# One 512-column pass for two halves: high weights meet the high and the low part of the activations together

## The reference

```python
def half_ffn(x, shift, scale, gate, g, w_gate, w_up, w_down):
    h = rmsnorm(x, g) * (1 + scale) + shift
    return x + 0.5 * gate * swiglu(h, w_gate, w_up, w_down)   # 1024 -> 2816 -> 1024
# layer 0: half_ffn, then Fourier and neighbourhood attention with w_out, then half_ffn
# layer 1: half_ffn, then latent (MLA) attention with w_o, then half_ffn; rmsnorm at the end
x_l = x_l + mod_l[:, 5] * y_l          # y_l = concatenated heads @ w_out, or @ w_o
```

## Time and profile before

| | us |
|---|---|
| median of 3 runs | 3292.5 (3287.77 to 3293.3) |
| the profiled execution, its own time | 3279.74 |
| its span, first to last instruction | 3277.6 |
| PE busy in the span | 2987.5 |
| DVE busy | 2356.1 |
| ACT busy | 1022.8 |

### The profile page before, as it was taken

One profiled execution on the slowest core, in us unless ns is written; L12 is line 12 of the kernel. 1 busy time (PEld: TensorE's weight loads), 2 busy tenths in 40 slices (PEclk: granted clock), 3 DMA queues, 4 the chain that ended last, 5 costly groups with the idle time before them and its releaser, 6 DMA issues. The chain is left out here.

```text
span 3277.6 us, 43558 instructions
## 1 busy us (share of the span) xinstructions
PE 2987.5 (91%) x15744; PEld 2395.9 (73%) x15744; DVE 2356.1 (72%) x4780; ACT 1022.8 (31%) x2039; POOL 1290.9 (39%) x1213
## 2 busy tenths in 40 slices
PE   8999899886877999989987999859999999999999
PEld 5877566564644587757665776639997999996898
DVE  5776777777877776787777877777754887846574
ACT  2423211111231242231111111135455544444443
POOL 1105777776767211577666666660000010000000
PEclk9999999998888999989998999969999999999999
DMA  9659999999999867999999999987661787742352
GB/s 352 226 200 370 377 409 409 409 409 385 395 352 389 333 231 269 368 381 409 409 406 408 395 409 409 404 321 239 225 226 42 256 278 242 254 156 90 123 182 102
DMA packets 276501, 1003.55 MB, mean 306 GB/s; under 512 B 31952, under 2 KB 32752, under 8 KB 276032
## 3 DMA queue, kind: packets, MB, share of 16 engines
q0 software_dynamic: 173696, 635.85, 50.5%
q1 hardware_dynamic: 100944, 361.15, 30.9%
q10 hardware_dynamic: 1648, 3.78, 0.3%
HBM read 999.57 MB, written 1.05 MB: 305 GB/s over the span
## 5 line engine op out<-in xcount | busy, mean ns | idle before, releaser
L288 PE MATMUL bank<-hT,ring 128*128 128x256 f32 x3744 | 838.5, 382 | 10.0 <-ACT hT L928 7.2
L288 PEld LDWEIGHTS bank<-hT,ring 128*128 128x128 f32 x3744 | 716.0, 192 | 139.3 <-issue 33.0
L414 POOL DMA_INDIRECT gring<-in_expert_u,idx x512 | 592.6, 1157 | 307.3 <-issue 146.5
L414 POOL DMA_INDIRECT gring<-in_expert_v,idx x512 | 599.9, 1172 | 277.1 <-issue 146.1
L584 PE MATMUL bank<-gring,dg 128*128 128x512 f32 x1012 | 526.0, 666 | 140.3 <-DMA gring<-in_expert_v,idx 121.2
L1387 DVE CUSTOM_DVE_ANT_0 gring<-gring,t_tok 128x1024 f32<-128x1024 f32 x512 | 601.2, 1222 | 20.2 <-DMA gring<-in_expert_u,idx 10.6
L1362 DVE SCALAR_TENSOR_TENSOR x<-gring,wts,x 128x1024 f32<-128x1024 f32 x259 | 333.0, 1286 | 279.0 <-DMA gring<-in_expert_v,idx 169.9
L1696 DVE TENSOR_TENSOR wl<-ring,wr 128x1024 fp32r<-128x1024 f32 x309 | 377.5, 1223 | 211.2 <-ACT wr L1691 210.7
L584 PEld LDWEIGHTS bank<-gring,dg 128*128 128x128 f32 x1012 | 209.7, 214 | 393.9 <-issue 359.4
L1700 PE MATMUL bank<-hr,wr 128*128 128x258 f32 (+1 forms) x1512 | 430.0, 284 | 1.5 <-DVE hl L2165 0.7
L1702 PE MATMUL bank<-hr,wl 128*128 128x258 f32 (+1 forms) x1512 | 426.6, 282 | 0.0
(11 more groups left out here) (327 smaller groups left out, 3697.7 us busy)
## 6 DMA issues: line engine op xcount, KB each, us to landing
ring<-in_stream SPq DMA_DIRECT2D x679, 512.0 KB
lat_ada<-in_ada POOLq DMA_DIRECT2D x66, 512.0 KB, 5.3
t_tok<-in_ada POOLq DMA_DIRECT2D x56, 512.0 KB, 5.2
gring<-in_ada POOLq DMA_DIRECT2D x56, 512.0 KB, 5.8
gring<-in_expert_u,idx POOLq DMA_INDIRECT x512
gring<-in_expert_v,idx POOLq DMA_INDIRECT x512
na_bias_sb<-in_na_bias POOLq DMA_DIRECT2D x1, 4096.0 KB, 15.2
x<-in_x SPq DMA_DIRECT2D x2, 512.0 KB, 4.3
```

What stands on the lines that cost most here:

```text
L288: last = pe.matmul(out, w[:, k * P:(k + 1) * P], act_T[:, k, :], start=(k == 0), stop=(k == KD - 1))
L414: pool.indirect_dma_start(out=gring[:, N % GR, :], out_offset=None, in_=table, in_offset=bass.IndirectOffsetOnAxis(ap=idx[:, b, 4 * (Q % 3 ...
```

## The change

The two matmuls that use `wr` are made one. High and low parts of an activation become halves of one tile (`hh0`, `hh1`, `ff`), and `pe_pair` sends both, 512 columns, through one matmul into a whole bank: high in columns 0 to 255, low in 256 to 511. The third matmul (`wl` x high) adds into columns 0 to 255. The residual then adds both halves: first gate x columns 256 to 511, then, after a wait on the semaphore `l_part`, gate x columns 0 to 255. Only the down and output projections use `pe_pair`; the projections behind a norm, and the ones in MLA's query, keep `pe_three`.

```diff
         def dve_residual(dve, R, m):
...
-            dve.scalar_tensor_tensor(out=hT[:, m, :], in0=bank[4 + m % 2][:, 0:S],
-                                     scalar=mods[:, L, (3 * j + 2) * KD + m, LAT:LAT + 1], in1=hT[:, m, :], op0=ALU.mult,
-                                     op1=ALU.add).then_inc(l_res, 1)
+            gate = mods[:, L, (3 * j + 2) * KD + m, LAT:LAT + 1]
+            dve.scalar_tensor_tensor(out=hT[:, m, :], in0=bank[4 + m % 2][:, S:2 * S], scalar=gate, in1=hT[:, m, :],
+                                     op0=ALU.mult, op1=ALU.add).then_inc(l_part, 1)
+            dve.wait_ge(l_part, 8 * R + m + 1)
+            dve.scalar_tensor_tensor(out=hT[:, m, :], in0=bank[4 + m % 2][:, 0:S], scalar=gate, in1=hT[:, m, :],
+                                     op0=ALU.mult, op1=ALU.add).then_inc(l_res, 1)
...
+        def pe_pair(pe, bk, s, i, both, start, stop):
+            cols = slice(i * P, (i + 1) * P)
+            pe.matmul(bk[:, :].rearrange("p (two t) -> p two t", two=2), wr[:, s % SPLIT, cols], both[:, :, 0:S], start=start,
+                      stop=False)
+            return pe.matmul(bk[:, 0:S], wl[:, s % SPLIT, cols], both[:, 0, 0:S], start=False, stop=stop)
...
-                    last = pe_three(pe, bank[4 + m % 2][:, 0:S], s0 + 44 + d, i, fr[:, k, :], fl[:, k, :], k == 0, k == KF - 1)
+                    last = pe_pair(pe, bank[4 + m % 2], s0 + 44 + d, i, ff[:, k], k == 0, k == KF - 1)
...
-                    hi, lo = (yr[:, k, 0:S], yl[:, k, 0:S]) if k < 4 else (hr1[:, k - 4, 0:S], hl1[:, k - 4, 0:S])
-                    last = pe_three(pe, bank[4 + st % 2][:, 0:S], LAB_O + st, k, hi, lo, i == 0, i == KD - 1)
+                    last = pe_pair(pe, bank[4 + st % 2], LAB_O + st, k, hh1[:, (k + 4) % KD], i == 0, i == KD - 1)
...
-                pe_unit_three(pe, M_O + st, bank[4 + st % 2][:, 0:S], [hr1[:, k, 0:S] for k in range(KD)],
-                              [hl1[:, k, 0:S] for k in range(KD)])
+                pe.wait_ge(w_low, M_O + st + 1)
+                for k in range(KD):
+                    last = pe_pair(pe, bank[4 + st % 2], M_O + st, k, hh1[:, k], k == 0, k == KD - 1)
+                last.then_inc(sp_used, 1)
...
-        hr0 = sb(ctx, "hr0", [P, KD, SX], F32R)
-        hl0 = sb(ctx, "hl0", [P, KD, SX], F32R)
+        hh0 = sb(ctx, "hh0", [P, KD, 2, SX], F32R)
...
-            fr = sb(for_ffn, "fr", [P, KF, S], F32R)
-            fl = sb(for_ffn, "fl", [P, KF, S], F32R)
+            ff = sb(for_ffn, "ff", [P, KF, 2, S], F32R)
```

More of the change, by code:

```diff
@@ L1727, in pe_normed_unit @@
         def pe_normed_unit(pe, n, u, out):
-            pe_unit_three(pe, u, out, [high[n][:, k, :] for k in range(KD)], [low[n][:, k, :] for k in range(KD)])
-        def pe_unit_three(pe, u, out, a_high, a_low):
             pe.wait_ge(w_low, u + 1)
             for k in range(KD):
-                last = pe_three(pe, out, u, k, a_high[k], a_low[k], k == 0, k == KD - 1)
+                last = pe_three(pe, out, u, k, high[n][:, k, :], low[n][:, k, :], k == 0, k == KD - 1)
             last.then_inc(sp_used, 1)
@@ L2232, in program @@
             "mla_roped", "mla_kv_mm", "mla_kv"))
-        stored, l_fin = sem("stored"), sem("lat_weighted")
+        stored, l_fin, l_part = sem("stored"), sem("lat_weighted"), sem("lat_residual_low")
         a_or, ab_yl, m_cr, m_cl = (sem(n) for n in ("att_out_high", "fft_low", "mla_cq_high", "mla_cq_low"))
@@ L2246, in program @@
             lat_ada = sb(for_condition, "lat_ada", [P, 4, UW])
-        hr1 = sb(ctx, "hr1", [P, KD, SX], F32R)
-        hl1 = sb(ctx, "hl1", [P, KD, SX], F32R)
+        hh1 = sb(ctx, "hh1", [P, KD, 2, SX], F32R)
+        hr0, hl0, hr1, hl1 = hh0[:, :, 0, :], hh0[:, :, 1, :], hh1[:, :, 0, :], hh1[:, :, 1, :]
         late = {n: sb(ctx, n + "_sb", list(io[n].shape)) for n in ("mla_gq", "rope", "rotm", "final_g")}
@@ L2267, in program @@
             turned = sb(for_mla, "turned", [P, 2, S])
+        fr, fl = ff[:, :, 0, :], ff[:, :, 1, :]
         lab_u, lab_q, lab_k = lab[:, 0:4, :], lab[:, 4:12, :], lab[:, 12:16, :]
```

## The result

The changed kernel takes 3299.5 us (median of 20 runs, 3288.6 to 3306.8), the kernel before 3291.4 (20 runs, 3282.7 to 3299.1). The ratio is 1.0024 with a 95% interval of 1.0015 to 1.0034. In microseconds that is +8.2 where +5.5 was forecast: slower, by a little more than the 6.6 us set as the mark for "no measurable change", and the interval lies on both sides of that mark. It is also just above the +3 to +8 us that the forecast gave itself, and inside its whole range (3286 to 3309).

The account below looks back on a forecast made before the run. PE was taken to bound down projections F = 0, 2 and 3, DVE F = 1, a DVE-ACT residual chain the output projections. 13.0 us for 25 residuals minus 7.5 (616 x) gave +5.5, 3298 us; range 3286 to 3309.

Parts of the forecast that it names:

- The residual's chains: Output projections: a chain round DVE and ACT, once a tile, goes from 3.85 to 4.37 us with the second residual instruction.
- the steep price: Rival: the 512-column matmul leaves one column a cycle, 60 ns lost on each product, about +50 us; chance 0.03.
- x: What one product saves on PE in down and output projections: 12.1 ns, from 356.3 to 344.2 ns.
- The residual, 25 times 0.52 us: Down and output projections: 25 residuals on the path, each 0.52 us longer as two dependent instructions, 13.0 us.
- I take 12.1 ns as paid once by each matmul: Products in down and output projections: fixed 12.1 ns a matmul beyond its columns, so a 512-column pass takes 225.4 ns.
- The two columns more of the earlier trace: 258-column matmuls start 119.6 ns apart, against 118.75 at 256: 0.85 ns for two columns, read as a cycle each.
- rival of a cost by columns: Rival: the pass costs by its columns, 235 ns, x = 2.6, +11.4 us; chance 0.25 together with nothing saved.
- The buffers are the same bytes in another order ... cost nothing: Moved tiles: no DMA, wait or copy added on ACT, SP or POOL, weights still early; cost nothing.
- the hidden load: Rival: weight load was the limit and is now hidden, pass 216 ns, x = 21.5, -0.2 us; chance 0.18.
- a change that does nothing (x = 0): Rival: three passes' worth of time in two instructions, +13.0 us, 3305.5; within the 0.25 for columns or nothing saved.
- a residual pair that overlaps: Rival: residual pair costs 0.40 us, with x = 21.5 gives -3.2 us; chance 0.06 for faster by 3 or more.

Follow-up runs that it names:

- the reordered kernels: ACT's weight copy moved earlier: output projections only, kernel before 0.9978, changed 0.9977; down projections and last tiles too, three matmuls 0.9959, change in most tiles 0.9932.
- tiles alone: Kernel before with only the change's tiles (high and low part as halves of one tile), three matmuls and one residual instruction kept; ratio 0.9990.
- changed, one residual instruction: Changed kernel without the residual instruction that adds columns 256 to 511; ratio 0.9982, latent stream 14.8 us under the changed kernel.
- halves apart: Changed kernel with the down projections' activations in rows of 258 columns, 256 used, so halves aren't side by side; latent stream 1079.4 us, not timed as ratio.
- changed kernel reordered: Changed kernel with ACT's weight copy ahead of the high part and square in both output projections; ratio 0.9977.
- fewer columns: Changed kernel, down projections' pass at 512, 512, 384, 320 columns in F = 0 to 3; pass means 230.5, 173.1, 145.1 ns at 512, 384, 320; no ratio.
- F = 1 and the last tiles freed too: Copy moved ahead in down and output projections, last tile's residual earlier, change's tiles; against kernel before 0.9959 with three matmuls, 0.9932 with the change except each stage's last tile.

## Why the prediction was right or wrong

The forecast was +5.5 us with a range that holds the result. The residual's chains, the main cost, were right; PE's gain was mis-sized, and the moved tiles were put at nothing. The range is as wide as all the rivals but the steep price, so that it held says little. By stage, each from the end of one stage's last residual to that of the next (starts read from both traces); the forecast from the prediction's own terms with x = 12.1 ns:

| | forecast | measured |
|---|---|---|
| up and down projection F = 0 | -1.6 | -1.9 |
| layer 0's mixer and output projection | +4.1 | +4.0 |
| F = 1 | +2.2 | +1.9 |
| F = 2 | -1.6 | -1.2 |
| MLA and its output projection | +4.1 | +5.6 |
| F = 3 and the end | -1.6 | -1.2 |
| sum | +5.5 | +7.2 |

*The residual, 25 times 0.52 us.* Right in its size (3089.03 to 3089.54, then 3090.06) and its places: 4.37 us a tile as predicted, the stretch of F = 1 at 38.10 with 38.1 predicted, PE's idle time behind a down projection up by 0.54. Shown from both sides, by adding an instruction to the kernel before (+11.8 for a cheaper one) and taking it from the changed one (-14.8, of which 1.5 is the clock). That the cause is the chain and not DVE's load is shown by the reordered kernels, for the output projections and for F = 1.

*"I take 12.1 ns as paid once by each matmul".* This step failed. The pass takes 230.6 ns and not 225.4, the matmul behind it 120.3 and not 118.75, and x is 4.8 (0.42 us in 88 products of F = 0) to 5.1. The two columns more of the earlier trace rows were too short a lever: over the whole stream 258 columns take 120.1 ns on the mean and in the new tiles 119.2, so place alone moves that distance by as much as the two columns were to show. A fixed price came out near the means at 320 and 384 columns, but not at 512, and at 384 it is 8 ns in one pattern and 21 in the other. With x = 4.8 the prediction's sum gives 13.0 - 3.0 = +10.0 us, near the rival of a cost by columns (+11.4 at 2.6 ns), which had 235 ns for the pass. The measured 230.6 lies halfway between the two.

*"The buffers are the same bytes in another order ... cost nothing".* This failed too, in the other direction. The new tiles alone make the stream 2.3 us shorter, 0.87 in each up projection, none of which has an edited instruction. In the changed kernel, whose down projections no longer have the matmuls that the new place slows, the placement is worth 4 x 0.87 = 3.5 us, and the sum is 10.0 - 3.5 = 6.5. The two errors, 4.5 us too much gain on PE and 3.5 us of placement not seen, have opposite signs. That the total came within 2 us of the measured one is in good part luck.

*The granted clock, 0.7 us.* Between 6.5 and the measured 7.2 lies the granted clock, which is not the same in the two executions. The MLA stage took 1.5 us more than forecast. None of its own instructions differ but the output projection's. Its stretches at a clock of 0.50 (1.2 GHz; columns as in the earlier trace rows) are one in the kernel before and two in the changed one. The one before, and the second of the changed one, come at the end of an idle time of PE of 4.26 us or just behind it; the first of the changed one is behind F = 2.

```profile
2973.20:2976.60 3.40, 3.27 (x4) 1.51 (x5) 1.12 (x4) 0.60 (x1) 0.00 (x0) 0.50 0.00 0
```

```profile
2951.20:2954.60 3.40, 3.40 (x18) 3.40 (x18) 0.06 (x1) 0.00 (x0) 0.00 (x0) 0.50 0.39 146
2992.10:2995.50 3.40, 3.40 (x6) 1.69 (x5) 0.62 (x3) 1.19 (x2) 0.00 (x0) 0.50 0.00 0
```

The stage's length goes with them in the other kernels too, when 8 x 0.52 = 4.2 us is taken off where the residual has two instructions:

| | stage, us | less residual | at 0.50, us |
|---|---|---|---|
| before | 142.9 | 142.9 | 3.4 |
| changed, one residual instruction | 142.9 | 142.9 | 3.4 |
| tiles alone | 144.2 | 144.2 | 6.8 |
| changed | 148.6 | 144.4 | 6.8 |
| halves apart | 149.4 | 145.2 | 10.2 |

In the four kernels with another order it is 138.1 us with 3.4 at 0.50, 139.9 and 140.0 with 6.8, and 140.5 with 10.2.

So the 1.5 us are the clock's. In the other direction, the stream's first 10 us had a mean granted clock of 0.74 before and 0.82 in the changed kernel, an estimated 0.8 us less (10 x 0.08). 6.5 + 1.5 - 0.8 = 7.2.

*What stays open.* In the changed kernel PE is idle 1.82 us behind F = 2, busy again from 2950.79, and its clock falls at 2951.20. It falls in that place in the other kernels with this idle time or more too (halves apart and the changed kernel reordered, 1.83 and 1.82 us; fewer columns, 2.74). Before, PE is idle 1.28 us there, and with the added residual instruction alone 1.74, and in neither does the clock fall there. It doesn't either behind F = 0 in the changed kernel, after the same 1.82. So the MLA stage's 1.5 us may belong to the change, by way of the longer idle time; no run tests it. Nor is the cause of the beat known, or why the new tiles speed up the products of 258 columns.

The rivals: the hidden load (216 ns) and the steep price fall by the 230.6 ns; a change that does nothing (x = 0) falls by the 0.42 us that the pass saves in F = 0's stretch; a residual pair that overlaps falls because its second half starts after the end of the first (3089.54, and 3089.03 + 0.48). The cost by columns has the wrong price for the pass, and its total of +11.4 would have been nearer to the +10.0 that the residuals and the true x give than the forecast was.

The Trainium skill's rule for the isolated distance ("TensorE: Matmul & The Clock Gate", "Back-to-back issue gap") would have 216 ns at 512 columns; the fp32r pass measured here, 224 to 235 ns and 230.6 on the mean, does not follow it.

## What to carry to other kernels

Before merging matmuls, count what the merge adds on the engine that reads the result, and walk the chain there: an instruction of half a microsecond costs its full time wherever tiles hand over one by one, and nothing beside a bound engine. Here 832 saved matmuls, worth 5 ns each, were paid with 25 such instructions. If the chain is the bound, first take out of it what needn't be there (the weight copy in front of `wl`); the merge pays only after that. Here it took all three places: with the output projections alone in the new order the change still gave nothing in the timed ratios, and with F = 1 and the last tiles freed too it gave some 3.4 to 4.6 us.

## What the runs showed of the hardware

- An fp32r matmul with its own weight load costs more than its columns at 2.4 GHz, and not by a fixed amount: 256 columns 118.7 ns on the mean, 320 from 140 to 153, 384 either 168 or 181, 512 224 to 235. Which of the values holds can change where an fp32 matmul has come between, with the same tiles and lengths. Plain fp32 records of 256 columns (L288) had 215 or 216 ns nearly throughout, where the granted clock was 1.00.
- Two tiles woven into one, with the same instructions, changed the 258-column products by 0.75% (115.27 to 114.40 us for 320 of them), the same 0.87 us in each of the four up projections and in all eight kernels here that have these tiles. The 256-column products got slower in the same tiles (33.03 to 33.10 us for the stretch of F = 0 with 88 products).
- `scalar_tensor_tensor` on 128x256 from PSUM took 0.42 us with a constant scalar and 0.48 with one read from a tile.
- Short stretches at a granted clock of 0.50 came at different places in the latent stream of different kernels. F = 2's stage took 194.8 us with one (2742.5 to 2745.9, changed kernel reordered) and 193.2 without (changed kernel). Differences of 1 to 2 us between single executions can be this alone.
